# One inference step of a sparse-attention, mixture-of-experts trunk: token rows picked already turned, slot marks moved, and the last tile spread over 128 partitions

## The chip, the cores and the metric

The kernel runs on one core of one Trainium2 chip. The metric is the device time of one execution in microseconds (us). The core has a matrix engine (TensorE, PE in the profile, with its weight loads shown as PEld), a vector engine (VectorE, DVE), an activation engine (ScalarE, ACT), GpSimd (POOL) and a sync engine (SyncE, SP), which here issues nearly all transfers; 16 DMA engines carry them. Operands lie in SBUF, products of TensorE in PSUM, in eight banks of 128 partitions by 512 float32.

## The reference

One layer: RMSNorm, an input projection, two attention mixers, a merge and an output projection; then the part that the change touches, a mixture of experts with 4 of 32 experts for each token, and the final RMSNorm. There are 256 prompt tokens and 64 sample tokens of 1024 channels each.

```python
def moe_ffn(h, w_router, b_router, w_gate_up, b_gate_up, w_down, b_down):
    logits = (h @ w_router + b_router).astype(jnp.float32)
    top_val, top_idx = lax.top_k(logits, TOP_K)
    gates = jax.nn.softmax(top_val, axis=-1)
    ...
    def expert_block(args):
        x_e, e = args
        gu = x_e @ w_gate_up[e] + b_gate_up[e]
        gate = jnp.minimum(gu[:, :D_FF], SWIGLU_LIMIT)
        up = jnp.clip(gu[:, D_FF:], -SWIGLU_LIMIT, SWIGLU_LIMIT)
        act = (up + 1.0) * gate * jax.nn.sigmoid(SWIGLU_ALPHA * gate)
        return act @ w_down[e] + b_down[e]
    ...
    return jnp.einsum('nk,nkd->nd', gates.astype(yb.dtype), y_assign.reshape(n, TOP_K, d))

x = x + moe_ffn(h, ...)        # residual, then:
y = x * rsqrt(mean(x*x) + 1e-5) * g      # the final RMSNorm, per token
```

All weights are float32. An expert has 8 MB of gate and up weights and 4 MB of down weights (1 MB is 2^20 bytes here), and each of the 32 is read once.

## The kernel before, in words

The tokens are held as three tiles: 0 and 1 with the prompt's 128 rows each, 2 with the 64 sample rows (`ROWS`). Each expert gets a block of 64 slots (`BS`); two experts make a pair, so there are 16 pairs (more only if an expert has over 64 tokens). The work of a pair `i` on TensorE is, in `pair(i)`:

- `gate_up(i, u)` for u = 0 and 1: eight steps over the channels; in each the 64 slots' turned rows `hTm` (stationary) meet 2048 weight columns. After every second step the semaphore `e_used` goes up by one: the 2 MB of weights behind those two steps are free. Bias products (L1519) end it.
- `picked(p)`: the rows of pair `p`'s 128 slots are picked out of the normed tokens `hn` by a product with the 0/1 matrix `pick` (L1480). Before, `pick` is stationary and `hn` moves, 512 columns at a time: 6 products, the result has slots on the partitions. ScalarE copies it to `hg` (`picked_out`), and `rows_t(p)` turns it on TensorE with eight 128x128 transposes (L1488), so that channels lie on the partitions; VectorE then scales it into `hTm` (`rows_out`).
- `down(i, u)`: eight steps over the hidden channels (L1540), with an `e_used` after four and after eight, then bias products (L1547).
- `acts_t` (L1527) turns the activations; `combine_first` and `combine_rest` (L1472, through `spread_out`) put the weighted expert outputs back to their tokens, and VectorE adds them to the residual `x5`. They need `ypair`, which ScalarE copies out of PSUM (`rows_y`, L1679 and L1680).

A float32 product is two instructions in the profile, each with its own weight load, so `picked` shows as 12, a pair's eight transposes as 8, `slot_marks` (L1496, twelve products of 52 columns) as 24.

`slot_marks` runs once, inside the first `down(0, 0)`: it finds which token and which gate weight belongs to each slot of each pair.

The order of the transfers is written out by hand in `sync_merge`. SP issues 2 MB transfers of weights in a fixed order, each after a wait on `e_used`: the number of the release that frees its place. Gate and up weights have one place of 8 MB for all experts, down weights two places of 4 MB. For expert 2's down weights SP waits for releases 9 and 10 (of `down(0, 0)`), for expert 3's gate and up weights 11 to 14 (of `gate_up(1, 0)`), for expert 3's down weights 15 and 16 (of `down(0, 1)`), for expert 4's gate and up weights from 17 on (of `gate_up(1, 1)`). Up to expert 17 (`FREED_PAIRS`, pair 8) transfers are issued in the order in which places come free; from pair 9 on in another order (`pair_weights`), whose first wait, release 101, comes from `gate_up(8, 1)`.

At the end `down(15, 1)` runs as its last weights land, the last `ypair` is copied, four spread products give the last sums (L1472), and the final norm follows per tile in the order 2, 0, 1: add (VectorE), squares summed (ScalarE), mean and epsilon (VectorE), root (ScalarE), reciprocal and scaling (VectorE, L2057 and L2063), store (SP).

Of the kernel before, what the change touches and what calls it, by code (L numbers as in the profile page):

```python
# [17 lines left out]
ALU = mybir.AluOpType  # L18
# [133 lines left out]
def build(nc, io, const_a, at_a, const_b, at_b):  # L152
    ctx = ExitStack()
    with ctx:
# [929 lines left out]
        hg, hTm = at(31232, D), at(26112, KD, 2 * BS)  # L1084
# [40 lines left out]
        at_slot = [at(31232, 8, 2 * BS), at(CONST_B + const_b.shape[1], 4, 2 * BS)]  # L1125
# [20 lines left out]
        pick_ready, pick_full, hg_ready = sem("pick_ready"), sem("pick_full"), sem("hg_ready")  # L1146
# [13 lines left out]
        half_picked, HALF_PICKED, half_rows, HALF_ROWS = p_ready, len(UNITS), pj_out[0], 9  # L1160

# [42 lines left out]
        def sync_merge(sp):  # L1204
# [111 lines left out]
            for k, t in enumerate(LAST_TILES):  # L1316
                sp.wait_ge(out_ready, k + 1)
                sp.dma_start(yp[128 * t:128 * t + 128] if t < 2 else ys, x5[0:ROWS[t], t, :]).then_inc(stored, 16)
            sp.wait_ge(stored, n_stored + 48)
# [20 lines left out]
        def pe_merge(pe):  # L1340
# [189 lines left out]
            def down(i, u, between={}, final=False):  # L1530

                past(pe, a_out, i * 2 + (u + 1))
                for c in range(KD):
# [12 lines left out]
                for h in range(2):  # L1546
                    last = nc.tensor.matmul(bank(6 + u)[64 * h:64 * h + 64], bsel[u][0:96, 0:BS], bias16[0:96, 2 * D + 512 * h:2 * D + 512 * h + 512],  # L1547
                                            start=False, stop=True)
                last.then_inc(yb_full, 1)

            def marks_and_rows():

                slot_marks()
                picked(1)
# [14 lines left out]
            def pair(i):  # L1569
# [29 lines left out]
            down(0, 0, {3: marks_and_rows, 6: lambda: rows_t(1)})  # L1599
# [8 lines left out]
            spread_out(0, (6, 7)).then_inc(comb_full, 1)  # L1608
            for h in range(2):
                spread_out(1, (2, 3), (h,)).then_inc(comb_full, 1)  # L1610

        def act_merge(act, st):
# [42 lines left out]
            def picked_out(p):  # L1655

                act.wait_ge(pick_full, p)
                past(act, x_tp, p)
                for h in range(2):
                    A(hg[:, 512 * h:512 * h + 512], bank(h), ACT.Copy).then_inc(hg_ready, 1)  # L1660

# [26 lines left out]
            picked_out(1)  # L1688
# [3 lines left out]
            with act.Fori(1, more + (NE // 2 - 1)) as i:  # L1692
                acts_out(i - 1, 1)
                sigmoid(i, 0)
                picked_out(i + 1)
# [11 lines left out]
            rows_y(end, 0)  # L1707
            nc.scalar.activation(ssf[:, 8:9], ident[:, 0:1], ACT.Sqrt)
            past(act, yb_full, end * 2 + 2)
            A(ypair[64:128, 0:512], bank(7)[0:64], ACT.Copy).then_inc(y_ready, 1)  # L1710
            def square(k):
                act.wait_ge(sum_ready, k + 1)
                if k < 2:
                    t = LAST_TILES[k]
                    r = ROWS[t]
                    st(A(sqf[t][0:r], x5[0:r, t], ACT.Square, accum_out=ssf[0:r, t:t + 1]), sq8)
# [1062 lines left out]
```

## Time and profile before

| | |
|---|---|
| Median of 3 runs | 1412.5 us (1412.35, 1412.5, 1417.41) |
| The profiled execution's own time | 1412.28 us |
| Its span, first to last instruction | 1410.6 us |
| Granted TensorE clock | 0.998 of full speed |
| PE busy, of the span | 1375.3 us, 97% |
| DVE busy, ACT busy | 467.4 us (33%), 285.5 us (20%) |
| Moved by DMA | 509.39 MB, mean 361 GB/s |
| Largest groups of the chain of waits | gate and up products 25%, down products 11%, DMA of gate and up weights 10%, `picked` 6%, DMA of down weights 5% |

The chain of waits is followed back from the last instruction: at each step to what released it. Its shares say what ended last, not what would be saved: where an engine runs without a pause beside a transfer stream that also never pauses, the chain can follow either. The stage of the experts begins at about 486 us and ends with the last down products at 1396 us.

### The profile page before, as it was taken

What the parts mean: (1) busy time and instruction counts of PE and PEld (TensorE: products, weight loads), DVE (VectorE), ACT (ScalarE), POOL (GpSimd) and SP (SyncE); (2) the same over time, 40 slices, a digit from 0 to 9 for tenths busy, and PEclk for the clock granted to TensorE, in tenths of its full rate; (3) what the DMA queues carried; (4) which work ended last, traced back from release to release, by engine and by line L of the source; (5) the groups of instructions that cost most, each with busy time, mean ns of one, the idle gap of its engine ahead of it and who ended that gap; (6) DMA issues with size and microseconds to landing.
All of it is one profiled execution on the core that took longest, in us unless ns stands there. A gap on an engine that the chain in (4) does not pass through costs nothing.

```text
span 1410.6 us, 19613 instructions
## 1 busy us (share of the span) xinstructions
PE 1375.3 (97%) x7357; PEld 602.3 (43%) x7357; DVE 467.4 (33%) x1025; ACT 285.5 (20%) x611; POOL 99.2 (7%) x220
## 2 busy tenths in 40 slices
PE   9999999999999999999999999999999999999987
PEld 4445556777754533333333333333333333333322
DVE  1115484665437432313313213132121231321314
ACT  3005434555541301001101010000101011001002
POOL 2000223434200000000000000000000000000000
PEclk9999999999999999999999999999999999999999
DMA  7336857999998699999999999999999999999995
GB/s 274 119 119 217 277 120 245 328 293 308 359 277 318 282 427 392 423 430 428 428 429 428 428 429 428 428 429 427 429 429 427 429 429 428 429 428 428 429 427 241
DMA packets 75516, 509.39 MB, mean 361 GB/s; under 512 B 19114, under 2 KB 25746, under 8 KB 46130
## 3 DMA queue, kind: packets, MB, share of 16 engines
q1 hardware_dynamic: 60978, 476.30, 83.1%
q0 software_dynamic: 13472, 28.87, 6.4%
q10 hardware_dynamic: 1024, 3.67, 0.7%
q8 instruction: 25, 0.41, 0.1%
q14 instruction: 17, 0.14, 0.0%
HBM read 502.29 MB, written 10.62 MB: 364 GB/s over the span
## 4 chain that ended last, share of the span: by engine, by line
PE 78%; DMA 17%; issue 2%; DVE 2%; ACT 1%; SPq 1%; DVEq 0%; POOL 0%; POOLq 0%; ACTq 0%
PE PS L1510 25%; PE PS L1540 11%; DMA arena<-in_w_gate_up 10%; PE PS L1480 6%; PE PS L367 5%; DMA arena<-in_w_down 5%; PE PS L2232 4%; PE PS L1472 4%; PE PS L630 3%; PE PS L616 3%; PE PS L1367 2%; PE PS L1179 2%; PE PS L382 1%; DMA arena<-in_cache_diff_k 1%; PE PS L1527 1%
## 5 line engine op out<-in xcount | busy, mean ns | idle before, releaser
L1510 PE MATMUL PS<-arena 128*64 128x512 f32 x2048 | 455.8, 595 | 12.2 <-DMA arena<-in_w_gate_up 12.1
L1510 PEld LDWEIGHTS PS<-arena 128*64 128x64 f32 x2048 | 141.5, 137 | 293.6 <-issue 263.8
L1540 PE MATMUL PS<-arena 128*64 128x512 f32 x1024 | 227.1, 594 | 2.7 <-DMA arena<-in_w_down 2.6
L1974 DVE TENSOR_SCALAR arena<-PS 128x512 f32<-128x512 f32 x32 | 22.1, 691 | 444.2 <-PE PS L1519 443.2
L1540 PEld LDWEIGHTS PS<-arena 128*64 128x64 f32 x1024 | 71.6, 137 | 150.7 <-issue 143.5
L1480 PE MATMUL PS<-arena 128*128 128x512 f32 (+1 forms) x180 | 84.2, 608 | 0.0
L1472 PE MATMUL PS<-arena 128*128 128x512 f32 (+1 forms) x192 | 79.4, 617 | 4.5 <-ACT arena L1680 3.7
L367 PE MATMUL PS<-arena 128*128 128x512 f32 (+1 forms) x192 | 77.3, 562 | 1.3 <-DMA arena<-in_w_in 1.3
L1891 DVE TENSOR_TENSOR arena<-PS,arena 128x512 f32<-128x512 f32 (+1 forms) x33 | 22.0, 671 | 167.2 <-PE PS L1488 166.7
L1328 POOL COPY arena<-arena 96x64 bf16 (+1 forms) x34 | 7.9, 234 | 985.8 <-PE PS L1547 941.2
L1665 ACT ACTIVATE arena<-arena 128x512 f32<-128x512 f32 x32 | 20.1, 630 | 266.3 <-DVE arena L1974 266.3
L1672 ACT ACTIVATE arena<-PS 128x512 f32<-128x512 f32 x32 | 19.1, 597 | 251.4 <-PE PS L1527 251.4
L630 PE MATMUL PS<-arena 128*128 128x252 f32 x256 | 68.1, 382 | 0.0
L616 PE MATMUL PS<-arena 128*128 128x128 f32 (+1 forms) x456 | 65.6, 277 | 1.8 <-DMA arena<-in_cache_diff_k 1.5
L1679 ACT ACTIVATE arena<-PS 64x512 f32<-64x512 f32 x31 | 18.3, 590 | 222.9 <-PE PS L1547 222.9
L616 PEld LDWEIGHTS PS<-arena 128*128 128x128 f32 (+1 forms) x456 | 53.1, 141 | 16.4 <-issue 6.1
L2232 PE MATMUL PS<-arena 128*128 128x512 f32 x128 | 59.9, 601 | 0.0
L886 ACT ACTIVATE arena<-PS 128x512 f32<-128x512 f32 (+5 forms) x96 | 44.6, 492 | 58.5 <-PE PS L616 56.4
L367 PEld LDWEIGHTS PS<-arena 128*128 128x128 f32 x192 | 36.1, 190 | 41.1 <-issue 38.0
L1480 PEld LDWEIGHTS PS<-arena 128*128 128x128 f32 (+1 forms) x180 | 31.6, 188 | 46.0 <-issue 45.9
L630 PEld LDWEIGHTS PS<-arena 128*128 128x128 f32 x256 | 42.7, 190 | 4.6 <-issue 1.5
L1472 PEld LDWEIGHTS PS<-arena 128*128 128x128 f32 (+1 forms) x192 | 24.9, 171 | 43.9 <-issue 36.9
(299 smaller groups left out, 1271.2 us busy)
## 6 DMA issues: line engine op xcount, KB each, us to landing
arena<-in_w_gate_up SPq DMA_DIRECT2D x128, 2048.0 KB, 20.0
arena<-in_w_down SPq DMA_DIRECT2D x62, 2048.0 KB, 21.8
arena<-in_cache_diff_k SPq DMA_DIRECT2D x64, 256.0 KB, 6.1
arena<-in_cache_diff_v POOLq DMA_DIRECT2D x64, 256.0 KB, 5.1
arena<-in_w_in SPq DMA_DIRECT2D x7, 2048.0 KB, 12.6
arena<-in_cache_cmp_kv POOLq DMA_DIRECT2D x64, 128.0 KB, 3.9
arena<-in_cache_sel_kv SPq DMA_DIRECT2D x64, 128.0 KB, 7.0
arena<-in_w_out SPq DMA_DIRECT2D x1, 4096.0 KB, 14.2
```

Of the source, the lines that this page charges most:

```text
L367: last = nc.tensor.matmul(bank(proj_bank(q, 2 * s + t))[:, 0:w], xnT[:, k, 128 * t:128 * t + 128], chunk_at(j)[:, k, 0:w], start=(k == 0), ...
L616: last = nc.tensor.transpose(place[0:c, col:col + r], src, ident[0:r, 0:r])
L630: last = nc.tensor.matmul(hidden_at[c], w1[:, c, l, :], cmp_window(c, l), start=(l == 0), stop=(l == CB // 2 - 1))
L886: copy = lambda d, s: nc.scalar.activation(d, s, ACT.Copy)
L1179: last = nc.tensor.matmul(bank(BRANCH_BANK[v][half])[p:p + r], src[:, k, 128 * t:128 * t + r], w[:, k, 512 * nh:512 * nh + 512], start=(k ...
L1367: last = nc.tensor.matmul(bank(Z_BANK[v])[p:p + r], mT[:, k, 128 * t:128 * t + r], w_out[:, k, 512 * nh:512 * nh + 512], start=(k == 0), s ...
L1472: last = nc.tensor.matmul(out, spread[:, 128 * t:128 * t + ROWS[t]], ypair[:, 512 * h:512 * h + 512], start=True, stop=True)
L1480: last = nc.tensor.matmul(bank(h), pick[0:ROWS[t], t], hn[t][0:ROWS[t], 512 * h:512 * h + 512], start=(t == 0), stop=(t == 2))
L1510: last = nc.tensor.matmul(bank(2 + role + 2 * u)[64 * h:64 * h + 64], hTm[:, k, BS * u:BS * u + BS], rows[:, D * role + 512 * h:D * role + ...
L1540: last = nc.tensor.matmul(bank(6 + u)[64 * h:64 * h + 64], aT[u][:, c % 4, 64 * (c // 4):64 * (c // 4) + 64], down_w[u][c // 4][:, c % 4, ...
L1974: st(V.tensor_scalar(g1, bank(2 + 2 * u), LIM, None, ALU.min), g1_ready)
L2232: last = nc.tensor.matmul(bank(7), xnT[:, k, 128 * t:128 * t + 128], chunk_at(j)[:, k], start=(k == 0), stop=(k == KD - 1))
```

## The change

1. **Rows picked turned.** `picked` takes `hn` as stationary operand in chunks of 128 channels and moves the 128 columns of `pick`: for each of 8 chunks three products, over tiles 0, 1 and 2 with 128, 128 and 64 rows. The result is turned already. `rows_t`, ScalarE's two copies to `hg` and the semaphores between them go.
2. **Slot marks.** `slot_marks` stands behind `down(0, 0)` instead of in its middle, and VectorE makes the marks `at_slot` after the first activation (`swiglu(0, 0)`) instead of before it.
3. **Spreads.** In `pair(i)`, `combine_first(i)` stands after the second step of `gate_up(i, 1)` instead of ahead of it.
4. **The end.** The last `down` makes its bias products in the middle. The sample tile's final norm works on 128 partitions by 512 columns: ScalarE copies the residual and the norm weights to that shape beforehand, the sums of squares of a token's two halves are joined by four one-column products (L1606 of the new kernel), ScalarE scales and SP stores two halves. Mean and epsilon go into ScalarE's root as scale and bias.

```diff
             def picked(p):
                 pe.wait_ge(pick_ready, p + 3)
-                for t in range(3):
-                    for h in range(2):
-                        last = nc.tensor.matmul(bank(h), pick[0:ROWS[t], t], hn[t][0:ROWS[t], 512 * h:512 * h + 512], start=(t == 0), stop=(t == 2))
-                last.then_inc(pick_full, 1)
-
-            def rows_t(p):
                 for k in range(KD):
-                    if k % 4 == 0:
-                        pe.wait_ge(hg_ready, p * 2 + (k // 4 - 1))
-                    last = nc.tensor.transpose(bank(k // 4)[:, 128 * (k % 4):128 * (k % 4) + 128], hg[:, 128 * k:128 * k + 128], ident)
+                    for t in range(3):
+                        last = nc.tensor.matmul(bank(k // 4)[:, 128 * (k % 4):128 * (k % 4) + 128], hn[t][0:ROWS[t], 128 * k:128 * k + 128], pick[0:ROWS[t], t],
+                                                start=(t == 0), stop=(t == 2))
                 last.then_inc(x_tp, 1)
...
-                                                down_w[u][c // 4][:, c % 4, 512 * h:512 * h + 512], start=(c == 0), stop=False)
-                    if c % 4 == 3:
+                                                down_w[u][c // 4][:, c % 4, 512 * h:512 * h + 512], start=(c == 0), stop=(final and c == KD - 1))
+                    if c == 3 or (c == KD - 1 and not final):
                         last.then_inc(e_used, 1)
...
                 picked(i + 1)
                 down(i - 1, 1)
-                rows_t(i + 1)
-                combine_first(i)
-                gate_up(i, 1, {3: lambda: acts_t(i, 0)})
+                gate_up(i, 1, {1: lambda: combine_first(i), 3: lambda: acts_t(i, 0)})
...
-            down(0, 0, {3: marks_and_rows, 6: lambda: rows_t(1)})
+            down(0, 0, {3: lambda: picked(1)})
+            slot_marks()
...
+            pe.wait_ge(sq8, 1)
+            for p in range(2):
+                for q in range(2):
+                    last = nc.tensor.matmul(bank(4)[64 * p:64 * p + 64, 0:1], ident[:, 64 * q:64 * q + 64], ssf[:, 2:3], start=(q == 0), stop=(q == 1))
+            last.then_inc(comb_full, 1)
             for h in range(2):
                 spread_out(1, (2, 3), (h,)).then_inc(comb_full, 1)
...
-            picked_out(1)
             rows_y(0, 0)
...
+            act.wait_ge(comb_added, end * 4)
+            for h in range(2):
+                A(x5h[64 * h:64 * h + 64], x5[0:NS, 2, 512 * h:512 * h + 512], ACT.Copy).then_inc(halves_ready, 1)
+                A(nfin_h[64 * h:64 * h + 64], nfin[64 * h:64 * h + 64, 512 * h:512 * h + 512], ACT.Copy).then_inc(halves_ready, 1)
...
+            square(0, x5h, 0, ssf[:, 2:3])
+            act.wait_ge(comb_full, end * 3 + 3)
+            root(ssf[:, 5:6], bank(4)[:, 0:1], eps8)
+            square(1, x5[:, 0], 0, ssf[:, 0:1])
+            act.wait_ge(sq8, 2)
+            root(ssf[:, 3:4], ssf[:, 0:1], eps8)
...
+            act.wait_ge(rstd8, ENDED + 2)
+            st(A(wh, wh, ACT.Copy, scale=ssf[:, 5:6]), sample_out)
...
+            st(V.tensor_tensor(x5h, x5h, bank(0), ALU.add), sum_ready)
+            st.own()
+            st(V.tensor_tensor(wh, x5h, nfin_h, ALU.mult))
```

TensorE's order at the first `down` (before, L1540 is `down`, L1496 `slot_marks`, L1480 `picked`, L1488 `rows_t`, L1510 `gate_up(1, 0)`):

```order
L1540 MATMUL PS<-arena 64x512 x8
L1496 MATMUL PS<-arena 128x52 x12
L1480 MATMUL PS<-arena 128x512 x6
L1540 MATMUL PS<-arena 64x512 x6
L1488 MATMUL PS<-arena 128x128 x8
L1540 MATMUL PS<-arena 64x512 x2
L1547 MATMUL PS<-arena 64x512 x2
```

The same place in the changed kernel (L1539 is `down`, L1486 `picked`, L1495 `slot_marks`):

```order
L1539 MATMUL PS<-arena 64x512 x8
L1486 MATMUL PS<-arena 128x128 x24
L1539 MATMUL PS<-arena 64x512 x8
L1547 MATMUL PS<-arena 64x512 x2
L1495 MATMUL PS<-arena 128x52 x12
```

Between the first and the second half of `down(0, 0)` there stand now 24 products of 128 columns, and neither slot marks nor transposes; the slot marks lie behind its end.

The end of TensorE's program, from the last half of the last `down` on, before (L1472 is `spread_out`):

```order
L1540 MATMUL PS<-arena 64x512 x16
L1547 MATMUL PS<-arena 64x512 x2
L410 ISA
L410 REGISTER_ALU
L1472 MATMUL PS<-arena 64x512 x2
L1472 MATMUL PS<-arena 128x512 x4
```

And in the changed kernel (L1478 is `spread_out`):

```order
L1539 MATMUL PS<-arena 64x512 x8
L1547 MATMUL PS<-arena 64x512 x2
L1539 MATMUL PS<-arena 64x512 x8
L410 ISA
L410 REGISTER_ALU
L1478 MATMUL PS<-arena 64x512 x2
L1478 MATMUL PS<-arena 128x512 x2
L1606 MATMUL PS<-arena 64x1 x4
L1478 MATMUL PS<-arena 128x512 x2
```

The bias products have moved ahead of the last four steps, and four one-column products stand ahead of tile 1's spreads.

## Rows read from the trace of the kernel before

**Rows 1.** The page, part 2: GB/s moved in 40 equal slices.
```profile
GB/s 274 119 119 217 277 120 245 328 293 308 359 277 318 282 427 392 423 430 428 428 429 428 428 429 428 428 429 427 429 429 427 429 429 428 429 428 428 429 427 241
```

**Rows 2.** Stretches: busy time by engine; the last three are clock, DMA share, GB/s.
```profile
530.00:536.00 6.00, 6.00 (x34) 2.46 (x32) 3.66 (x12) 1.19 (x2) 0.23 (x1) 1.00 0.67 224
600.00:800.00 200.00, 198.96 (x866) 70.60 (x864) 47.13 (x93) 21.20 (x36) 1.64 (x7) 1.00 1.01 429
```

**Rows 3.** Chain of waits, 560 to 622 us: start, duration, what.
```profile
560.88 0.23 PE PS L1547 x2
562.38 1.98 PE PS L1472 x4
564.36 7.02 PE PS L1510 x32
...
620.55 1.86 PE PS L1510 x7
```

**Rows 4.** SP's DMA issues in time (x4: first of four).
```profile
519.90 0.33 SPq L1198 DMA_DIRECT2D arena<-in_w_down  x1
533.14 0.33 SPq L1198 DMA_DIRECT2D arena<-in_w_down  x1
536.79 11.46 SPq L1195 DMA_DIRECT2D arena<-in_w_gate_up  x4
557.48 3.76 SPq L1198 DMA_DIRECT2D arena<-in_w_down  x2
568.14 11.44 SPq L1195 DMA_DIRECT2D arena<-in_w_gate_up  x4
967.64 0.35 SPq L1195 DMA_DIRECT2D arena<-in_w_gate_up  x1
```

**Rows 5.** Us from issue to landing: issues at 519.90, 533.14, 536.79, 557.48, 568.14, 967.64.
```profile
arena<-in_w_down SPq DMA_DIRECT2D x1, 2048.0 KB, 14.3
arena<-in_w_down SPq DMA_DIRECT2D x1, 2048.0 KB, 8.3
arena<-in_w_gate_up SPq DMA_DIRECT2D x1, 2048.0 KB, 9.5
arena<-in_w_down SPq DMA_DIRECT2D x1, 2048.0 KB, 9.1
arena<-in_w_gate_up SPq DMA_DIRECT2D x1, 2048.0 KB, 8.3
arena<-in_w_gate_up SPq DMA_DIRECT2D x1, 2048.0 KB, 10.3
```

**Rows 6.** Chain of waits, 470 to 535 us (L1406: the first pick, turned too).
```profile
478.78 1.09 PE PS L1406 x8
...
480.88 1.87 PE PS L1406 x16
...
519.86 2.94 PE PS L1496 x24
522.80 5.54 PE PS L1480 x12
...
531.07 1.02 PE PS L1488 x8
```

**Rows 7.** Weight loads in time, 525 to 529 us; idle time before each in brackets.
```profile
525.41 0.19 PEld L1480 LDWEIGHTS PS<-arena 128*128 128x128 f32 x1 [0.24 <-issue]
526.36 0.29 PEld L1480 LDWEIGHTS PS<-arena 64*128 64x128 f32 x2 [0.76 <-issue]
526.89 0.19 PEld L1480 LDWEIGHTS PS<-arena 64*128 64x128 f32 x1 [0.24 <-issue]
527.32 0.19 PEld L1480 LDWEIGHTS PS<-arena 64*128 64x128 f32 x1 [0.24 <-issue]
```

**Rows 8.** The end of the chain of waits.
```profile
1358.68 33.56 DMA arena<-in_w_down
...
1395.94 0.23 PE PS L1547 x2
...
1402.88 1.27 DVE arena L2063
...
1406.28 1.28 DVE arena L2063
```

More of the change, by code:

```diff
@@ L1315, in sync_merge @@
             yp, ys = io["y_prompt"][0], io["y_sample"].rearrange("b t d -> (b t) d")
[L1316 to L1319, printed above, removed]
+            sp.wait_ge(out_ready, 1)
+            sp.dma_start(yp[0:128], x5[:, 0, :]).then_inc(stored, 16)
+            sp.wait_ge(sample_out, ENDED + 1)
+            for h in range(2):
+                sp.dma_start(ys[:, 512 * h:512 * h + 512], wh[64 * h:64 * h + 64]).then_inc(stored, 16)
+            sp.wait_ge(out_ready, 2)
+            sp.dma_start(yp[128:256], x5[:, 1, :]).then_inc(stored, 16)
+            sp.wait_ge(stored, n_stored + 64)
         def pool_moe(pool, st):
@@ L1545, in down @@
                         between[c]()
-                for h in range(2):
-                    last = nc.tensor.matmul(bank(6 + u)[64 * h:64 * h + 64], bsel[u][0:96, 0:BS], bias16[0:96, 2 * D + 512 * h:2 * D + 512 * h + 512],
-                                            start=False, stop=True)
+                    if c == (3 if final else KD - 1):
+                        for h in range(2):
+                            last = nc.tensor.matmul(bank(6 + u)[64 * h:64 * h + 64], bsel[u][0:96, 0:BS], bias16[0:96, 2 * D + 512 * h:2 * D + 512 * h + 512],
+                                                    start=False, stop=not final)
                 last.then_inc(yb_full, 1)
-            def marks_and_rows():
-                slot_marks()
-                picked(1)
             def combine_first(i):
@@ L1654, in act_merge @@
             st(A(gt, gt, ACT.Exp), gt_exp)
[L1655 to L1660, printed above, removed]
             def sigmoid(i, u):
@@ L1707, in act_merge @@
             rows_y(end, 0)
+            act.wait_ge(comb_added, end * 4)
+            for h in range(2):
+                A(x5h[64 * h:64 * h + 64], x5[0:NS, 2, 512 * h:512 * h + 512], ACT.Copy).then_inc(halves_ready, 1)
+                A(nfin_h[64 * h:64 * h + 64], nfin[64 * h:64 * h + 64, 512 * h:512 * h + 512], ACT.Copy).then_inc(halves_ready, 1)
             nc.scalar.activation(ssf[:, 8:9], ident[:, 0:1], ACT.Sqrt)
@@ L1941, in dve_merge @@
             op(V.scalar_tensor_tensor, slotn, pairn, -float(2 * BS), dflat, ALU.mult, ALU.add)
-            for a0, marks in zip((0, 8), at_slot):
-                n = marks.shape[1]
-                st(V.tensor_tensor(marks, iota.unsqueeze(1).to_broadcast([128, n, 2 * BS]), sf[:, a0:a0 + n].to_broadcast([128, n, 2 * BS]), ALU.is_equal))
             op(V.tensor_tensor, at_pair, dispatch_const("pair").unsqueeze(1).to_broadcast([128, 12, NBLK // 2]), pf.to_broadcast([128, 12, NBLK // 2]), ALU.is_equal)
@@ L2003, in dve_merge @@
             swiglu(0, 0)
+            for a0, marks in zip((0, 8), at_slot):
+                n = marks.shape[1]
+                before(V.tensor_tensor(marks, iota.unsqueeze(1).to_broadcast([128, n, 2 * BS]), sf[:, a0:a0 + n].to_broadcast([128, n, 2 * BS]), ALU.is_equal),
+                       marks_ready if a0 else None)
             swiglu(0, 1)
@@ L2032, in dve_merge @@
             end = more + (NE // 2 - 1)
+            st(V.memset(eps8, EPS))
             swiglu(end, 0)
@@ L2074, in dve_merge @@
                 v = x5[:, 1, 512 * h:512 * h + 512]
                 st(V.tensor_tensor(v, v, bank(2 + h), ALU.add), sum_ready)
-            variance(0)
-            final_norm(2)
+            last_rstd(2, 1)
+            last_rstd(0, 2)
             final_norm(0)
             dve.wait_ge(sq8, 3)
-            st(V.tensor_scalar(ssf[:, 6:7], ssf[:, 6:7], 1.0 / D, EPS, ALU.mult, ALU.add))
-            st.own()
-            variance(1)
+            st(V.tensor_scalar(ssf[:, 6:7], ssf[:, 6:7], 1.0 / D, EPS, ALU.mult, ALU.add), var8)
@@ L2083, in dve_merge @@
+            last_rstd(1, 3)
             final_norm(1)
```

68 lines of the change are left out of this document (21 added, 47 removed).

## The prediction

> **What bounds the kernel now.** I read the page's slices first. TensorE is busy in every slice, 97% of the span, which looks like the bound; but from slice 19 of the GB/s row to the last but one the rate stands at 427 to 430 without a dip [rows 1]. A rate that never moves is a limit, so I asked for stretches: from 600 to 800 us the DMA engines are busy all the time (share 1.01) at 429 GB/s [rows 2]. A transfer of 2048 KB (2.097 MB) takes 4.89 us at that rate, and a pair of experts, twelve of them, 58.7 us. TensorE needs less: in the chain a pair runs from 564.36 to 620.55, 56.19 us [rows 3]. The stream is the bound and TensorE has 2.5 us to spare in each pair. The chain names TensorE for most of this time because it never stands still long; its last long piece is a wait for a transfer, 33.56 us up to 1392.2 [rows 8].
>
> So three things can move the end: a pause in the stream, a stream that TensorE no longer keeps fed, and what follows the last landing. The stretch from 530 to 536 shows a pause: 224 GB/s [rows 2], so (429 - 224) x 6 / 429 = 2.9 us are lost. The issues explain it. A transfer lands 8.3 us after its issue when the queue is empty (seen at 533.14 and 568.14), else 4.89 us after the one ahead of it [rows 4, 5]. The one issued at 519.90 lands at 534.2; the next, released by the second half of the first `down`, is issued at 533.14 only and lands at 541.4 where 539.1 was possible. Those of 536.79, 557.48 and 568.14 land at 546.3, 566.6 and 576.4: each just as the queue runs out or within a microsecond of it. For the first two pairs the stream is only as early as TensorE's releases; later the queue is deep.
>
> **Rows picked turned.** It takes away a 5.54 us `picked` and 1.02 us of transposes [rows 6], and adds 24 products of 128 columns, 48 instructions. The first pick does the same product (L1406): 16 instructions in 1.87 us, 0.117 each; the group of 8 with 64 rows takes 1.09 [rows 6]. But the new loop goes over the tiles innermost, with 128, 128, 64 rows, so it changes between 128 and 64 rows 16 times per `picked`, where before there were two (into tile 2 and out of it). What a change costs stands in the weight loads of `picked`: 0.43 us from one to the next (526.89 to 527.32), but from 525.41 to 526.36 it is 0.95 for two, 0.09 too much, and from 526.36 to the next slot at 526.89 it is 0.53, 0.10 too much [rows 7]. The next load waits until the array is free instead of running ahead. I take 0.19 a change. It fits twice: 12 x 0.43 + 2 x 0.19 = 5.54, and the 64-row group, which has one change in all (half going in, half going out), leaves (1.09 - 0.19) / 8 = 0.1125 for an instruction [rows 6]. The new `picked` is then 48 x 0.1125 + 16 x 0.19 = 8.4 us; with 0.117 each it is 8.65. I take 8.5, 2.95 more than now. Bounds: no cost of changes beyond today's, 48 x 0.1125 + 0.4 = 5.8 (+0.3); changes at 0.23 with 0.117 each, 9.3 (+3.8).
>
> **Slot marks and the first releases.** Going through the issues of [rows 4] in order:
> - Release 10 (533.14): slot marks (2.94) and transposes (1.02) [rows 6] no longer stand before it, 2.95 is added: 532.1, landing 540.4, now 541.4.
> - Release 11 (536.79): the marks are back ahead of `gate_up(1, 0)`, so -1.02 + 2.95: 538.7, landing 547.0 (546.3 now). The three behind it land by 561.7.
> - Release 15 (557.48): a second `picked` stands before it: +1.93 + 2.95 makes 562.4, landing 570.7, where it is 566.6 now. The queue is empty for 4 us. Release 16's lands at 575.6.
> - Release 17 (568.14): +4.88, less the 1.27 between bias products and spreads (561.11 to 562.38: transposes and the wait for ScalarE's copy) and less the 1.98 of `combine_first`, which stands behind this release now [rows 3]: 569.8. It lands at 580.4, now 576.4. The stream is 4.0 us late.
>
> So the slot marks' move alone would gain, and the dearer `picked`, counted twice before release 15, takes more than that. VectorE's marks after `swiglu(0, 0)` cost nothing: VectorE waits there for the products of the next half, and `slot_marks` comes later than before. ScalarE's removed copies lay beside products.
>
> **The later pairs.** A pair on TensorE becomes 56.19 + 2.95 - 1.27 = 57.9 us, still under the stream's 58.7, so no pair by itself costs anything; but the spare grows by 0.8 us a pair instead of 2.5. That matters at pair 8, where the order of transfers changes and the two of expert 17's down weights are held back: there the landing of the issue at 967.64 takes 10.3 us, only 2.0 above the empty queue's 8.3 [rows 4, 5]. After the change: release 101 comes seven pairs after release 17, at 569.8 + 7 x 57.9 = 975.1, so it cannot land before 983.4. Between them stand 84 - 2 = 82 transfers: 580.4 + 82 x 4.89 = 981.4. Late by 2.0. The next release has `combine_first` ahead of it (3.4 + 2.0 = 5.4 against 4.89), 0.5 more. I take 2.5. From there on the spare grows again, and `last_pair` has no `picked`, so the last landing is the stream's. Sum for the stream: 4.0 + 2.5 = +6.5, less 0.2 for small losses now right behind 568.14, which a fuller queue avoids: +6.3.
>
> **The end.** The bias products leave the last `down`: -0.23. VectorE no longer scales the sample tile in the chain: -1.27 [rows 8]. Against this four one-column products (8 instructions of at most 0.117, and two changes of column count, which I price as the row changes at 0.19) delay tile 1's sums by up to 1.3; half of it lies beside VectorE's addition of tile 0, so I take +0.7. Two more, smaller stores go out while tile 1 is scaled. Sum -0.8, bounds -1.5 and +0.5.
>
> **Sum.** 1412.28 (the profiled execution, 0.2 under the median of 1412.5) + 6.3 - 0.8 = 1417.8; with the 0.2 to the median, 1418.0.
>
> **Rivals.**
> - *Weight loads run ahead across a change of rows in short products.* Then `picked` becomes 6.0 us (+0.5). Release 15 moves by -1.02 + 1.0 and its landing stays at 565.8 or better; release 17's then lands at 565.8 + 2 x 4.89 = 575.6 instead of 576.4, 0.8 earlier, the spare keeps growing (a pair is 55.4), and the end gives 0.8: 1412.5 - 1.6 = 1410.9, not slower. For it: three first-pick groups ran at 0.117 to 0.136 an instruction. Against: the 0.76 of idle time before the 64-row load [rows 7]. It decides if `picked` stays under 6.5 us (+0.9: release 15 comes 2 x 0.9 - 1.02 = 0.8 later, which eats the gain). The Trainium skill (TensorE: Matmul & The Clock Gate, Part 2: What happens when you issue a matmul) says that TensorE pulls a weight load ahead of running products if the row groups don't conflict or it goes to the background buffer. By the second half of that rule this rival would hold; the trace shows it between equal rows only.
> - *The pause at pair 8 doesn't come.* If TensorE's pair is 57.6 or less, 7 x 0.3 = 2.1 of the 2.5 go: 1418.0 - 2.3 = 1415.7. My 57.9 is a sum of four rows; this is within its error.
> - *Changes cost more in groups of two instructions* (+3.5): twice 0.55 more at release 15, and the pair 58.4, 7 x 0.55 more at pair 8: 1418 + 1.1 + 3.9 = 1423.
> - *TensorE is the bound after all*, as its 97% suggest: 14 pairs x 1.7 = 24 us, 1436. Against it stands the flat 429 GB/s.
>
> **How the numbers follow.** Forecast 0.53 (own range 1416.2 to 1419.9), loads run ahead 0.17, no pause at pair 8 0.15, dearer changes 0.12, TensorE the bound 0.03. What a measurement can tell from no change is about 0.5%, 7.1 us: beyond 1419.6 or below 1405.4. Slower by that: the last two cases and 0.07 of the forecast's, 0.22. Faster: 0.02, for something not seen here. Within: 0.76. The range goes from 1410.7 to 1422.0.
>
> **What would show it.** In the changed profile: `picked` (L1486) at 8.5 us for 48 instructions, its weight loads with a gap every four and every two; the issue of the second half of expert 2's down weights at 532, that of expert 3's at 562.4 with 8.3 us to its landing; a dip in the GB/s there and a small one near 980; a pair of 57.9 us on TensorE early on; the last scaling 6 us later than now. A `picked` under 6.5 us would make the forecast wrong, as would PE waiting for nothing but itself near the end.

## The result

| | before | after |
|---|---|---|
| Median of 6 runs each | 1413.01 us (1412.35 to 1417.41) | 1418.51 us (1417.95 to 1423.28) |
| Ratio after to before | | 1.0039, 95% interval 1.002 to 1.0057 |
| The profiled execution's own time, its span | 1412.28, 1410.6 us | 1419.65, 1418.0 us |
| First `gate_up` product of the stage | 486.36 us | 489.13 us |
| Last landing of weights | 1394.68 us | 1402.70 us |
| From there to the end of the span | 15.9 us | 15.3 us |

The changed kernel is 0.4% slower, 5.5 us by the medians. Of the 7.4 us between the two spans 2.8 stand ahead of the change: the stage of the experts begins that much later in this one execution. TensorE waits 1.5 us longer there for the attention part's cache transfers (3.3 instead of 1.8); where the rest comes from isn't shown. In the ten profiles of this study the stage began between 486.4 and 489.1 us, with no order by kernel, so I count it as chance and measure everything from the stage's beginning. The stage up to the last landing takes 913.57 instead of 908.32 us, +5.25, and what follows takes 0.6 less.

The page after, engines and GB/s in 40 slices, answers to [rows 1]:

```profile
PE 1400.7 (99%) x7785; PEld 657.3 (46%) x7785; DVE 466.2 (33%) x1022; ACT 271.9 (19%) x586; POOL 99.1 (7%) x220
...
GB/s 273 119 118 219 277 114 256 330 293 302 340 272 320 280 427 342 426 429 429 428 429 429 428 428 428 428 428 413 430 428 428 429 428 428 429 428 429 428 428 251
```

Where before one slice was low in this stage (392), there are now two, 342 and 413: one at the first pairs and one at pair 8. All the rest is at the stream's limit as before. The stretches after, answering to [rows 2] (the last number is GB/s, the one before it the DMA share):

```profile
533.00:540.00 7.00, 7.00 (x46) 4.05 (x44) 1.79 (x8) 1.28 (x3) 0.23 (x1) 1.00 0.89 335
558.00:572.00 14.00, 14.00 (x70) 5.98 (x69) 0.69 (x1) 1.18 (x2) 0.23 (x1) 1.00 0.76 297
600.00:800.00 200.00, 200.00 (x956) 82.72 (x952) 45.91 (x92) 15.96 (x27) 1.56 (x7) 1.00 1.01 429
975.00:990.00 15.00, 15.00 (x69) 5.01 (x65) 1.22 (x1) 0.60 (x1) 0.00 (x0) 1.00 1.01 395
```

The chain of waits after, first pairs (start, duration, what), answering to [rows 3, 6]:

```profile
522.63 8.45 PE PS L1486 x48
...
552.97 8.45 PE PS L1486 x48
...
568.66 3.44 PE PS L1509 x16
572.09 1.92 PE PS L1478 x4
...
626.41 3.44 PE PS L1509 x16
```

`picked` is 8.45 us long each time. A pair on TensorE goes from 568.66 to 626.41, 57.75 us (56.19 before), 0.95 under the stream's 58.7. Whether TensorE then has that much to spare is seen from its waits. Those from 486 us on (in total, times, longest), before, here for transfers of weights alone:

```profile
PE PS L1510 <- DMA arena<-in_w_gate_up: 12.1, 17, 1.2
PE PS L1540 <- DMA arena<-in_w_down: 2.6, 3, 1.2
```

And after, all of them:

```profile
PE PS L1478 <- DVE arena L2035: 0.9, 1, 0.9
PE PS L1412 <- DVE arena L1839: 0.7, 1, 0.7
```

The first of these two lies behind the last `down` product, the second ahead of the first `gate_up` product. Between them, in 914.8 us, the view lists no wait for weights. What it can't list, short waits and those inside a group of products, is about 0.3 us, all in the last 12 us: 0.1 at 1392.8, and 0.2 in the last group of `down` products, which takes 3.64 us where an unhindered one takes 3.44. Before, TensorE waited 14.7. What that means is taken up behind the experiments.

SP's issues after, answering to [rows 4]:

```profile
534.71 0.33 SPq L1200 DMA_DIRECT2D arena<-in_w_down  x1
541.45 11.46 SPq L1197 DMA_DIRECT2D arena<-in_w_gate_up  x4
565.05 3.76 SPq L1200 DMA_DIRECT2D arena<-in_w_down  x2
...
976.56 5.83 SPq L1197 DMA_DIRECT2D arena<-in_w_gate_up  x2
```

And the time from issue to landing of the first transfer of each of these four, answering to [rows 5] (the last number, us):

```profile
arena<-in_w_down SPq DMA_DIRECT2D x1, 2048.0 KB, 7.7
arena<-in_w_gate_up SPq DMA_DIRECT2D x1, 2048.0 KB, 8.4
arena<-in_w_down SPq DMA_DIRECT2D x1, 2048.0 KB, 7.6
arena<-in_w_gate_up SPq DMA_DIRECT2D x1, 2048.0 KB, 9.0
```

A pause of the stream is the time from one landing to the next beyond the 4.89 us of a full queue; pauses are named by the issue of the transfer that lands late. Those of the 2 MB transfers issued from 500 us on are: 0.5 at the issue of 534.71, 2.5 at 541.45, 3.3 at 565.05 and 1.4 at the one behind it, 0.4 at 976.56 and 0.65 at the one behind it; with the small ones 9.15 us. Before they are 3.33 us.

The end of the chain after, answering to [rows 8]:

```profile
1400.33 3.64 PE PS L1539 x16
...
1404.82 2.99 PE PS L1478 x8
1407.81 0.34 PE PS L1606 x8
...
1412.93 1.28 DVE arena L2043
```

### The profile page after: what moved, and what is told of

It reads as the page before. It is cut to its first block, busy times and chain, and to the rows that moved or that the text cites. A ratio compares the mean times of both kernels' runs of the same rounds, so it can differ in the third digit from the quotient of the medians.

```text
span 1418.0 us, 20386 instructions
## 1 busy us (share of the span) xinstructions
PE 1400.7 (99%) x7785; PEld 657.3 (46%) x7785; DVE 466.2 (33%) x1022; ACT 271.9 (19%) x586; POOL 99.1 (7%) x220
## 4 chain that ended last, share of the span: by engine, by line
PE 89%; DMA 5%; DVE 3%; issue 1%; ACT 1%; SPq 1%; DVEq 0%; POOLq 0%; ACTq 0%; POOL 0%
PE PS L1509 31%; PE PS L1539 15%; PE PS L1486 9%; PE PS L367 5%; PE PS L1478 5%; PE PS L2211 3%; PE PS L630 3%; PE PS L616 3%; PE PS L1373 2%; PE PS L1181 2%; DMA arena<-in_w_down 2%; DMA arena<-in_cache_diff_k 2%; PE PS L382 1%; PE PS L1526 1%; PE PS L2173 1%
## 5 line engine op out<-in xcount | busy, mean ns | idle before, releaser
L1539 PE MATMUL PS<-arena 128*64 128x512 f32 x1024 | 226.5, 594 | 0.1
L1539 PEld LDWEIGHTS PS<-arena 128*64 128x64 f32 x1024 | 72.0, 137 | 137.9 <-issue 133.4
L1486 PE MATMUL PS<-arena 128*128 128x128 f32 x720 | 127.9, 308 | 0.0
L1486 PEld LDWEIGHTS PS<-arena 128*128 128x128 f32 x720 | 97.9, 188 | 33.7 <-issue 6.6
L1671 ACT ACTIVATE arena<-PS 64x512 f32<-64x512 f32 x31 | 18.2, 589 | 332.1 <-PE PS L1547 332.1
L1478 PE MATMUL PS<-arena 128*128 128x512 f32 (+1 forms) x192 | 79.6, 618 | 0.9 <-DVE arena L2035 0.9
L367 PE MATMUL PS<-arena 128*128 128x512 f32 (+1 forms) x192 | 77.3, 562 | 0.9 <-DVE arena L2576 0.9
L2009 DVE TENSOR_TENSOR arena<-arena,PS 128x1024 f32<-128x1024 f32 x14 | 17.1, 1221 | 166.5 <-PE PS L1478 166.5
L1664 ACT ACTIVATE arena<-PS 128x512 f32<-128x512 f32 x32 | 19.1, 597 | 231.9 <-PE PS L1526 231.9
L616 PEld LDWEIGHTS PS<-arena 128*128 128x128 f32 (+1 forms) x456 | 53.0, 141 | 18.6 <-issue 6.0
L367 PEld LDWEIGHTS PS<-arena 128*128 128x128 f32 x192 | 36.1, 190 | 40.6 <-issue 38.0
L1478 PEld LDWEIGHTS PS<-arena 128*128 128x128 f32 (+1 forms) x192 | 24.8, 171 | 48.0 <-issue 48.0
## 6 DMA issues: line engine op xcount, KB each, us to landing
arena<-in_w_gate_up SPq DMA_DIRECT2D x128, 2048.0 KB, 15.3
```

The costliest lines, as they stand in the source:

```text
L367: last = nc.tensor.matmul(bank(proj_bank(q, 2 * s + t))[:, 0:w], xnT[:, k, 128 * t:128 * t + 128], chunk_at(j)[:, k, 0:w], start=(k == 0), ...
L616: last = nc.tensor.transpose(place[0:c, col:col + r], src, ident[0:r, 0:r])
L1478: last = nc.tensor.matmul(out, spread[:, 128 * t:128 * t + ROWS[t]], ypair[:, 512 * h:512 * h + 512], start=True, stop=True)
L1486: last = nc.tensor.matmul(bank(k // 4)[:, 128 * (k % 4):128 * (k % 4) + 128], hn[t][0:ROWS[t], 128 * k:128 * k + 128], pick[0:ROWS[t], t], ...
```

## The experiments

The theory: `picked` pays for each change between operands of 128 and of 64 rows. It makes the first releases late (two pauses) and takes most of TensorE's spare time per pair (a pause at pair 8), while the other parts are worth about nothing for this first and little for the end. Every kernel was timed with the kernel before on the same chip. The edits are to the changed kernel unless the text says otherwise.

**e1_snake: half of the changes.** The tiles in the order 0, 1, 2 and 2, 1, 0 in turn: 8 changes instead of 16, the same products.

```diff
                 for k in range(KD):
-                    for t in range(3):
+                    for n, t in enumerate((2, 1, 0) if k % 2 else (0, 1, 2)):
...
-                                                start=(t == 0), stop=(t == 2))
+                                                start=(n == 0), stop=(n == 2))
```

> The changed kernel with the tiles taken 0, 1, 2 for even chunks and 2, 1, 0 for odd ones in picked: the same 24 products, 8 changes between 128 and 64 rows instead of 16. Theory (each change of rows costs 0.19 us, and the time reaches the end through the stream's early pauses): picked 48 x 0.1125 + 8 x 0.19 = 6.9 us, the pause before expert 3's down weights shrinks from 4.7 us to about 2.5, none at pair 8; 4.5 us faster than the changed kernel, within 1 us of the kernel before (ratio 1.000 to 1.001). Rival A (the 48 weight loads cost the time, whatever their rows): picked stays 8.45 us, the time stays that of the changed kernel (1.004). Rival B (TensorE is the bound): 15 x 1.5 = 22 us faster than the changed kernel (0.988).

Measured: 1414.78 us, ratio 1.0007 (0.9998 to 1.0016). `picked` in the chain:

```profile
520.05 7.10 PE PS L1486 x48
```

8 changes less are 1.35 us less, 0.17 each. The stretch from 965 to 980 us moves 429 GB/s: no pause at pair 8. The pauses are 6.2 us. The time is in the range that was expected (1.000 to 1.001). Rival A, under which `picked` stays at 8.45 us, falls; so does rival B's 22 us, though not for the reason that TensorE had time to spare before this edit (see behind the experiments).

**e2_full_rows: no changes at all.** Tile 2 is used with all 128 rows; its rows 64 to 127 are set to zero once.

```diff
-                        last = nc.tensor.matmul(bank(k // 4)[:, 128 * (k % 4):128 * (k % 4) + 128], hn[t][0:ROWS[t], 128 * k:128 * k + 128], pick[0:ROWS[t], t],
+                        last = nc.tensor.matmul(bank(k // 4)[:, 128 * (k % 4):128 * (k % 4) + 128], hn[t][:, 128 * k:128 * k + 128], pick[:, t],
...
+            st.own()
+            st(V.memset(hn[2][64:128], 0.0))
```

> The changed kernel with tile 2 taken with all 128 rows in picked, its rows 64 to 127 set to zero once beforehand: the same 24 products, no change of rows inside. Theory: picked 48 x 0.1125 = 5.4 us, as much as the old form without the transposes; the stream's pauses shrink to 3 us in all and the time is 7.5 us below the changed kernel, 2 us below the kernel before (ratio 0.9985). Rival A: 8.45 us and 1.004. Rival B (TensorE bound): 15 x 3 = 45 us faster (0.97).

Measured: 1411.88 us, ratio 0.9987 (0.9978 to 0.9996; 0.9985 was expected), 6.6 us under the changed kernel's median, with more rows per product. (The two were timed on different occasions; by their ratios to the kernel before it is 7.3.) The weight loads of `picked` in the changed kernel, 522.5 to 531.2 us (busy, mean ns, idle before):

```profile
L1486 PEld LDWEIGHTS PS<-arena 128*128 128x128 f32 x32 | 4.2, 190 | 1.7 <-issue 0.8
L1486 PEld LDWEIGHTS PS<-arena 64*128 64x128 f32 x16 | 2.4, 184 | 1.0
```

The same 48 in e2_full_rows:

```profile
L1486 PEld LDWEIGHTS PS<-arena 128*128 128x128 f32 x48 | 5.4, 192 | 0.8 <-issue 0.8
```

And their piece of its chain:

```profile
520.10 5.55 PE PS L1486 x48
```

The 0.8 us is the wait ahead of the group. Within it the loads of the changed kernel stand idle for 1.9 us (1.7 + 1.0 - 0.8) and those of e2_full_rows never: there each load follows the last without a gap. The rest shows in the loads themselves, 6.6 us (4.2 + 2.4) against 5.4. 16 changes cost 8.45 - 5.55 = 2.90 us, 0.18 each. That the price falls in proportion to the changes (0, 8, 16: 5.55, 7.10, 8.45) shows that they are what costs, not the product's form, and not the 64-row products as such, of which e1_snake has all 8 of the changed kernel: in the turned form without changes `picked` takes what the old one took (5.54).

**e3_old_pick: the first part undone.** `picked` and `rows_t` as before (with ScalarE's copies), everything else as changed.

```diff
                 down(i - 1, 1)
+                rows_t(i + 1)
                 gate_up(i, 1, {1: lambda: combine_first(i), 3: lambda: acts_t(i, 0)})
...
-            down(0, 0, {3: lambda: picked(1)})
+            down(0, 0, {3: lambda: picked(1), 6: lambda: rows_t(1)})
             slot_marks()
```

> The changed kernel with the first part undone: the pick of before (pick stationary, 512 columns of rows moving), ScalarE's copy and the transposes are back; slot marks, spreads and the end are as changed. Theory: the slot marks' move shortens the pause at release 10 from 2.4 us to near nothing and opens one of 1.5 to 2 us at release 11 and about 1 at release 15: the stream ends where it did, the end gives 0.6: 0.5 us below the kernel before (0.9995), 6 below the changed one. Rival (another part makes the kernel slower, the end or the spreads): it stays above 1.002.

Measured: 1413.23 us, ratio 0.9996 (0.9987 to 1.0005). From its chain:

```profile
521.81 5.54 PE PS L1486 x12
...
563.18 1.02 PE PS L1494 x8
...
619.20 1.02 PE PS L1494 x8
```

Its pauses are 4.1 us, 0.5, 2.4 and 1.2 at the first pairs and none later. A pair on TensorE is 56.02 us (563.18 to 619.20), 0.17 less than before. The ratio is the expected one (0.9995), and the rival, above 1.002, falls. So parts 2 to 4 alone are no change that can be measured, and part 1 costs 5.3 us by the medians, 6.1 by the two ratios.

**e4_turned_only: the first part alone**, put into the kernel before; slot marks, spreads and the end stay where they were.

```diff
                 down(i - 1, 1)
-                rows_t(i + 1)
                 combine_first(i)
...
-            down(0, 0, {3: marks_and_rows, 6: lambda: rows_t(1)})
+            down(0, 0, {3: marks_and_rows})
...
-                picked_out(i + 1)
                 rows_y(i - 1, 1)
```

> The kernel before with only the first part: rows picked turned. Theory: picked 8.45 us; as slot marks still stand before release 10, the pause there grows to about 5 us, and with the one at release 15 the stream ends 6 to 7 us late; with the old end: 1.0045 to 1.005 of the kernel before. Rival (the parts only cost together): no more than 1.001.

Measured: 1437.46 us, ratio 1.0163 (1.0149 to 1.0177). This was a miss by three to four times, and it taught most. Its chain behind `down(0, 1)` (L1540 bias products, L1664 and L1665 ScalarE's copies of `ypair`, L1472 spreads, L1503 `gate_up`):

```profile
567.24 0.23 PE PS L1540 x2
...
568.10 0.60 ACT arena L1665
...
568.74 1.98 PE PS L1472 x4
570.72 7.02 PE PS L1503 x32
...
629.83 7.02 PE PS L1503 x32
```

From bias products to spreads 1.27 us pass, exactly as before, though the transposes are gone. The waits of PE from 600 to 1400 us (in total, times, longest), of e4_turned_only and then of the kernel before:

```profile
PE PS L1472 <- ACT arena L1665: 16.7, 13, 1.3
```

```profile
PE PS L1472 <- ACT arena L1680: 3.4, 13, 0.3
```

The 1.02 us of transposes had lain beside TensorE's wait for ScalarE's copy of `ypair`; without them the wait is 1.3 instead of 0.3. A pair on TensorE is then 570.72 to 629.83, 59.1 us: more than the stream's 58.7. TensorE is the bound: it waits for no transfer of weights from 486 us on, and its last `down` product ends 18.2 us later, from the stage's beginning, than the changed kernel's, about the 18.0 us of its 14 waits for that copy. Releases fall behind pair by pair, and the stream shows it:

```profile
985.00:1000.00 15.00, 15.00 (x73) 5.19 (x70) 1.07 (x2) 0.60 (x1) 0.00 (x0) 1.00 0.73 297
1000.00:1340.00 340.00, 332.30 (x1566) 134.77 (x1566) 84.40 (x174) 28.30 (x47) 2.79 (x12) 1.00 1.00 426
```

The queue has run down to nothing by pair 8 (a pause of 8.55 us there), and four later pairs have one of 0.7 to 1.6 each. The pauses are 23.7 us. They aren't the 24 us of the time: the last landing comes 19.6 us later than before, and from there to the end it takes 19.8 us instead of 15.9, as TensorE still has 5.2 us of its last `down` to do.

**e5_turned_spreads: parts 1 and 3**, to test that reading: e4_turned_only with `combine_first` behind the second step of `gate_up(i, 1)`, so that the copy lies beside products.

```diff
-                combine_first(i)
-                gate_up(i, 1, {3: lambda: acts_t(i, 0)})
+                gate_up(i, 1, {1: lambda: combine_first(i), 3: lambda: acts_t(i, 0)})
```

> The kernel before with the first part and the spreads' new place (combine_first behind the second step of gate_up). Theory on the 24 us of the kernel with the first part alone: its pair on TensorE is 59.1 us, above the stream's 58.7, as TensorE still waits 1.27 us for ScalarE's copy, a wait beside which the old transposes lay for nothing; with the spreads moved that wait is covered, the pair is 57.9, the queue keeps its depth, and the kernel is 5.5 to 6 us slower than before: ratio 1.004. Rival (the slot marks' place causes the 24 us): still about 1.016.

Measured: 1421.54 us, ratio 1.0056 (1.0037 to 1.0075). From its chain:

```profile
566.88 3.44 PE PS L1503 x16
...
624.63 3.44 PE PS L1503 x16
```

The wait is gone and the pair is 57.75 us, 1.36 less than e4_turned_only's. Neither step gives this alone: without the transposes, and the spreads where they were, a pair gains nothing (59.1 is 56.19 plus the 2.91 of `picked`); with the spreads moved and the transposes kept it gains 0.17 (e3_old_pick). By the medians 16 of e4_turned_only's 24 us go with one line. Its ten runs fall in two groups, five at a granted clock of 0.998 with 1417.15 to 1419.1 us and five at 0.992 with 1423.98 to 1427.47; the median lies between them, and that of the first five alone is 1417.56, 1.0026 of the kernel before. The ratio of all is 0.0016 over what was expected, which its interval still holds; the rival, 1.016, falls.

**e6_pick_behind_down: the release ahead of the pick.** `picked(i + 1)` stands behind `down(i - 1, 1)`, so releases 15 and 16 don't wait for it.

```diff
-                picked(i + 1)
                 down(i - 1, 1)
+                picked(i + 1)
```

> The changed kernel with picked(i + 1) behind down(i - 1, 1) instead of ahead of it. The release of expert 3's down weights no longer has the second picked before it: 553.9 instead of 562.4 in the time of the changed profile. Theory (releases through the queue, pair by pair): that pause goes, but release 17 comes no earlier and finds the queue empty, 1.5 to 2 us of pause there, and 2.5 to 3.5 at pair 8 instead of 1: the sum is the same, ratio to the kernel before 1.004 as the changed kernel. Rival (the pause at release 15 is what it costs): 4.7 us faster than the changed kernel, 1.0005.

Measured: 1418.66 us, ratio 1.0037 (1.0024 to 1.005): no difference from the changed kernel. Its stretches:

```profile
555.00:572.00 17.00, 17.00 (x87) 9.25 (x84) 0.69 (x1) 1.18 (x2) 0.23 (x1) 1.00 0.98 409
572.00:596.00 24.00, 24.00 (x110) 8.16 (x110) 10.82 (x24) 2.41 (x4) 0.23 (x1) 1.00 0.97 379
```

The pause at release 15 is gone (409 GB/s where the changed kernel has 297), and others stand up to 30 us later: 0.7 at 576.4, 0.7 at 580.7, 1.6 at 590.9. All pauses together are 9.4 us, 9.2 in the changed kernel. The work in front of a release can be reordered, but release 17 and those behind it still have the same products ahead of them. TensorE does the same work and again waits for no weights: to the end of its last `down` product it is 915.0 us, 914.8 in the changed kernel. Only less work helps.

**e7_order_kept_longer: the pause at pair 8.** The order of transfers changes at pair 12 instead of pair 8.

```diff
-        FREED_PAIRS = NE // 4
+        FREED_PAIRS = 3 * NE // 8
```

> The changed kernel with the order of transfers changed at pair 12 instead of pair 8 (FREED_PAIRS 12). Theory: the spare of the queue, growing by 0.8 us a pair, is 3 us larger by then, no pause at pair 8 and none at 12: 1.1 us faster than the changed kernel, 1.003 of the kernel before. Rival (the pause only moves): no gain, and GB/s dips near 1215 us.

Measured: 1420.72 us, ratio 1.0046 (1.0033 to 1.0059). Its stretches at pair 8 and pair 12:

```profile
972.00:990.00 18.00, 18.00 (x78) 6.17 (x76) 3.55 (x5) 1.23 (x2) 0.00 (x0) 1.00 1.00 424
1200.00:1215.00 15.00, 15.00 (x68) 5.19 (x66) 1.22 (x1) 1.78 (x3) 0.23 (x1) 1.00 1.00 426
```

In the profile the pause at pair 8 is gone (424 GB/s against 395) and none took its place at pair 12; up to the last landing the stage is 912.40 us, 1.2 under the changed kernel's 913.57. But the kernel gains nothing by it. From the last landing to the end it is 17.7 us instead of 15.3, since TensorE isn't there yet. The chain's last `down` products, after a last landing at 1399.03:

```profile
1399.27 3.46 PE PS L1539 x16
```

They end 3.7 us after that landing (1.27 in the changed kernel), and 916.1 us after the first `gate_up` product against 914.8. TensorE had no wait to give up, and the other order gives it two, at 1124.5 and 1183.3 us:

```profile
PE PS L1509 <- DMA arena<-in_w_gate_up: 1.2, 2, 0.8
```

The timed runs agree with no gain: 1.0046 against 1.0039, each within the other's interval. The expected 1.1 us took the end of the stream for the end of the kernel. The rival was right on the time and wrong on the reason: the pause went, and did not move.

**e8_all_rows_early_scale: the best of it together.** e2_full_rows with the order of e6_pick_behind_down, and ScalarE scales the sample tile ahead of tile 1's root.

```diff
-            act.wait_ge(var8, 1)
-            root(ssf[:, 4:5], ssf[:, 1:2], ssf[:, 6:7])
             act.wait_ge(rstd8, ENDED + 2)
             st(A(wh, wh, ACT.Copy, scale=ssf[:, 5:6]), sample_out)
+            act.wait_ge(var8, 1)
+            root(ssf[:, 4:5], ssf[:, 1:2], ssf[:, 6:7])
```

> A version meant to beat both: tile 2 with 128 rows in picked (no changes of rows), picked(i + 1) behind down(i - 1, 1), and the sample tile's scaling on ScalarE ahead of tile 1's root, so that its two stores are issued before tile 1 is ready. Theory: pauses after 490 us are 1 to 2 us in all, the stream ends 2.7 earlier than before, the end gives 0.6 and the stores 0.2 to 0.3: 3.6 us below the kernel before, ratio 0.9975. Rival (nothing is left to gain beyond the kernel with 128 rows): 0.9987.

Measured: 1411.0 us, ratio 0.9979 (0.9966 to 0.9993). It beats both kernels; from e2_full_rows (0.9987) it can't be told apart. The stage is 1.35 us shorter than before, where 2.7 were expected: from 490 us on its pauses are 3.6 us, not 1 to 2. VectorE's last scaling in the chain:

```profile
1405.47 1.28 DVE arena L2045
```

And SP's last issues, the sample's two stores and tile 1's:

```profile
1405.17 1.25 SPq L1322 DMA_DIRECT2D out_y_sample<-arena  x2
1406.79 0.35 SPq L1324 DMA_DIRECT2D out_y_prompt<-arena  x1
```

The last store goes out at 1406.79, as the scaling ends (1406.75), and no longer waits for the sample's two. From the last landing to the end it is 14.9 us, against 15.3 in the changed kernel.

**All profiles together, the stream's side.** From the stage's first product to the last landing, and the pauses in it (us):

| kernel | stage | pauses | stage less pauses |
|---|---|---|---|
| before | 908.32 | 3.33 | 904.99 |
| after | 913.57 | 9.15 | 904.42 |
| e1_snake | 911.22 | 6.18 | 905.04 |
| e2_full_rows | 908.08 | 3.32 | 904.76 |
| e3_old_pick | 908.33 | 4.08 | 904.25 |
| e4_turned_only | 927.89 | 23.65 | 904.24 |
| e5_turned_spreads | 913.99 | 9.90 | 904.09 |
| e6_pick_behind_down | 913.75 | 9.38 | 904.37 |
| e7_order_kept_longer | 912.40 | 8.20 | 904.20 |
| e8_all_rows_early_scale | 906.97 | 2.58 | 904.39 |

The last column stays within 0.95 us while the stage varies by 21. Most of that follows from how a pause is counted, so it says that the stream has a fixed length when nothing holds it up; it doesn't say which side makes the kernel wait. (A pause at the first issue of the stage, near 490 us, isn't in the table: 1.3 us before, 0.4 after, up to 1.6 in e1_snake.)

**TensorE's side.** From the same first product to the end of the last `down` product, and TensorE's waits for weights in it (us, as the view of waits lists them, so without the short ones; 0 where it lists none):

| kernel | to the last `down` product | waits for weights |
|---|---|---|
| before | 909.6 | 14.7 |
| after | 914.8 | 0 |
| e1_snake | 912.4 | 12.9 |
| e2_full_rows | 909.3 | 29.0 |
| e3_old_pick | 909.6 | 16.9 |
| e4_turned_only | 933.0 | 0 |
| e5_turned_spreads | 915.3 | 0.5 |
| e6_pick_behind_down | 915.0 | 0 |
| e7_order_kept_longer | 916.1 | 1.2 |
| e8_all_rows_early_scale | 908.2 | 29.5 |

Here the kernels fall into two groups. Where TensorE waits for weights by 12.9 us or more, the time depends little on its work: e1_snake and e2_full_rows take 20 and 43.5 us of `picked` out of the changed kernel (15 times 1.35 and 2.90) and gain 2.4 and 5.5. Where it doesn't wait, each microsecond of its path counts: e4_turned_only has 18.0 more and takes 18.2 longer. The changed kernel stands at the crossing. `picked` has used up all of TensorE's waits, so its stage lasts as long as TensorE's own products do, and the stream's pauses are what this looks like from the other side; the stream, for its part, ends just in time (0.3 us of wait). So less work on TensorE helps a little, more work costs in full, and a better order of transfers gives nothing.

## Why the prediction was right, step by step

Its sum was 1418.0 us against 1418.51 measured, +5.5 us by its medians and +5.5 by those measured. That they agree so well is in part luck: the profiled parts add up to 5.25 - 0.6 = 4.6, not 5.5; the first pairs cost 0.6 more than said, pair 8 1.4 less. Issues are given here less the 2.8 us by which this execution's stage began later.

- **What bounds it**: right before the change, only half right after it. The stream runs at 429 GB/s from 600 to 800 us, but TensorE never idles there either, and it waits for no weights in the whole stage. The spare of 0.8 us a pair is what its releases gain on the stream, not time in which TensorE stands still. The sum came out because it reaches release 101 by TensorE's pairs (569.8 + 7 x 57.9) and goes on by the stream only from there, where both sides come out the same: TensorE works for 427.4 us without a wait worth naming, and the stream needs 426.1 of them to its last landing and the last products 1.3 more. For the same reason the 4.0 us of the first pairs cancel in the forecast: they are in the landing at pair 8 either way. One of the prediction's own signs of being wrong, "PE waiting for nothing but itself near the end", came true but for the 0.3 us of the last 12. The rival "TensorE is the bound after all" named the engine; its price, 14 x 1.7 = 24 us, left out that TensorE could first use up the 14.7 us that it waited for weights. That e4_turned_only measured 1437.46, near the rival's 1436, is chance: its pair is 2.9 us longer than before, not 1.7.
- **`picked`**: 8.5 said, 8.45 measured; a change 0.19 said, 0.17 to 0.18 measured. The two gaps in [rows 7] had been enough to price it. The rival in which weight loads run ahead (6.0) fell. The Trainium skill (TensorEngine Tiling (Array Packing), Key Properties) says that changing the tiling mode drains the TensorE. The runs agree: with 16 changes the loads stand idle for 1.9 us, without any, in e2_full_rows, they never do and `picked` takes 5.55 us.
- **Release 10**: 532.1 said, 531.9 measured. **Release 11**: 538.7, 538.7. **Release 15**: 562.4, 562.3. **Release 17**: 569.8, 569.5. The landing of release 17's transfer: 580.4 said, 581.0 measured. The pauses at the first pairs add up to 7.7 us where the prediction's landings make 7.1. The 8.3 us for a transfer into an empty queue rested on a misreading: the one issued at 568.14 landed at 576.4, 4.89 after the one ahead of it (571.5), so the queue was not empty. Into an empty queue, at release 15, it took 7.6 us; against that, release 16's transfer had a pause of 1.4 where none was forecast.
- **A pair on TensorE**: 57.9 said, 57.75 measured. The working took it as the sum of four rows. Its term of -1.27 was about right as a sum, but "transposes and the wait for ScalarE's copy" were counted as two things that each go by themselves. Removing the transposes alone gives nothing (e4_turned_only), moving the spreads alone 0.17 us (e3_old_pick); together they give 1.36 (59.11 less 57.75). The prediction held because both parts were in the change.
- **Pair 8**: 2.5 said, 1.06 measured, the term most off. Release 101 came at 973.8, not 975.1 (seven pairs at 0.15 less, and 0.3 from release 17), and a full queue ahead of it would have run to 982.0 (581.0 + 82 x 4.89), not 981.4. That takes 1.9 of the 2.0 us; what stayed is a pause of 0.4, and 0.65 where 0.5 was said. It is a small difference of two numbers near 980: an error of 0.15 us per pair is 1 us of it. The measured pause lies between the forecast's and that of the rival without it (1415.7); the measured time is above both.
- **The stream**: +6.3 said, +5.25 measured: 0.6 more at the first pairs (4.6 late at release 17's landing, 4.0 said), 1.4 less at pair 8, 0.2 less in small losses.
- **The end**: -0.8 said, about -0.6 measured. The last scaling begins 10.2 us after the last landing (11.6 before), 1.37 earlier. Of this, 0.7 is lost again: the last scaling was over at 1414.21, but the last store went out only after the sample's two, and these wait for ScalarE's scaling, which stands behind tile 1's root. The timeline:

```profile
1412.60 0.71 ACT L1725 ACTIVATE arena<-arena 128x512 f32<-128x512 f32 x1
...
1412.93 1.28 DVE L2043 SCALAR_TENSOR_TENSOR arena<-arena 128x1024 f32<-128x1024 f32 x1
1413.34 1.17 SPq L1322 DMA_DIRECT2D out_y_sample<-arena  x2
1414.55 0.58 SPq L1324 DMA_DIRECT2D out_y_prompt<-arena  x1
```

  The prediction priced these two stores at nothing, since they "go out while tile 1 is scaled"; the last store is issued 0.3 after the scaling's end. The other 0.4 lies behind the issue (3.45 us to the end, 3.0 before), and no run tells why. The one-column products were priced too high: 8 instructions take 0.34 us, not 1.3.

What stays open: why the stage begins anywhere from 486.4 to 489.1 us (the attention part's transfers were not studied), why release 16's transfer had a pause of its own, and what set the granted clock of 0.992 in half of e5_turned_spreads's runs.

## What to carry to other kernels

When transfers bound a kernel, price each change by what it does to the releases that transfers wait for. Keep two ledgers, the stream's with its pauses and the engine's with its waits: more work costs little only while the engine still waits for data somewhere, and once those waits are used up the engine is the bound, even beside a stream that looks full. Work that lies beside a wait is worth nothing when it is removed, so look for what the engine would wait for next. Loops over operands of unequal height should change the height seldom (there and back, as in e1_snake), or pad the short one with zeros (e2_full_rows). A difference between two nearly equal rates (57.75 and 58.7 us here) must be known to a few tenths of a per cent before a pause can be computed from it.

## What the runs showed of the hardware

- A change between 128-row and 64-row operands costs 0.17 to 0.18 us in a float32 product of 128 columns (8.45, 7.10 and 5.55 us with 16, 8 and 0 changes), more than the 0.11 to 0.12 us of an instruction (5.55 / 48). Padded to 128 rows all 48 take 0.116 each, where the prediction had 0.1125 for one of 64 rows.
- Products of one column take 0.043 us an instruction (8 in 0.34), changes of column count included.
- A 2 MB transfer of weights issued with no other under way landed after 7.2 to 7.6 us (988.25 in e4_turned_only, 565.05 in the changed kernel). Issued 0.9 to 2.3 us before the last one ahead landed it took 7.7 to 8.4 (533.14 before; 534.71 and 541.45 after). In a full queue one landed every 4.89 us.
